# A third gate/up block multiplied plainly at the start of a float32 feed-forward layer

## The chip, the cores and the metric

The kernel runs on one core of a Trainium2 chip. A time is the device time of one execution in microseconds (us); of several runs the median is given. TensorE (PE in the profile) multiplies, PEld is its weight load, VectorE is DVE, ScalarE is ACT, GpSimd is POOL, and SyncE (SP) issues the loads of the weights.

## The reference, cut to what matters

One encoder layer on 512 tokens of width 2048 (forgetting attention, then a SwiGLU layer of inner width 5632), all in float32:

```
h = rmsnorm(x, norm_mix);  x = x + forgetting_attention(h)
h = rmsnorm(x, norm_ffn)
gu = h @ w_gate_up                    # 2048 x (2*5632)
x = x + (silu(gu[:, :5632]) * gu[:, 5632:]) @ w_down
out = rmsnorm(x, final_norm)
```

Only the line of `gu` is touched, and of it only the first 512 of the 5632 columns on each side.

## The kernel before, in words

Every float32 operand is held as a high and a low part in a rounded format. ScalarE copies the source into the high part, VectorE subtracts that from the source to get the low part, and TensorE adds three products: high by high, low by high, high by low. So each product of K-tiles is 3 matmuls, and each weight must pass through ScalarE and then VectorE before TensorE has the whole of it.

The feed-forward layer goes over 44 blocks of 128 inner columns, in 11 groups of 4. A group multiplies its four gate/up blocks and then adds the group's share of the down projection (16 output tiles, 192 matmuls of 512 columns). Groups 1 to 9 are a loop over `r`; group 0 is written out before it (`r is None`), the last behind it.

A block can be multiplied in three ways.
- `early` (L1604): block 0. Gate and up, each for one half of the tokens at a time, 48 matmuls of 256 columns. It needs nothing but the split weights in the two ring slabs of the phase before.
- `plain_part` (L1611): block 1. The block is cut into 4 parts (gate or up, first or second half of K); each part is 24 matmuls of 512 columns, 16 with the high weights and 8 with the low ones. 96 matmuls in all.
- `unit` with `half_product` (L1647, L1626): blocks 2 and 3, and every block of the later groups. The 2x2 form with seven products instead of eight. Weights B11, B12 (gate, up, first half of K) and B21, B22 (second half), tokens A11, A12, A21, A22 likewise. Each of the seven is 24 matmuls of 256 columns, so 168 in a unit. VectorE forms sums of weights in place in `raw` (`sum_of`), and the token sums S1 to S4 are formed once, before the first unit.

The token sums are made in pieces of 512 columns, four pieces for each: `sum_piece(i)` (VectorE from L1345, ScalarE from L944) makes piece i of S1, S2 and S3 and takes six additions or subtractions (L1338) and three low parts (L1343); ScalarE makes the high parts in between (L948, L950, L953). `fourth_piece(i)` makes piece i of S4 with 3 additions, a high part (L960) and a low part. All go through the same small tiles `sy`, `sz` and `qq`, so VectorE and ScalarE hand each piece back and forth.

The parts of the weights stand in a ring of two: part n may be written as a high part (ScalarE, L853, `part_hi`) once TensorE has read the highs of part n-2 (`highs_read`), as a low part (VectorE, L1217, `part_lo`) once part n-2 is done (`product`). The first two parts of the ring lie where block 0's gate slab was, and wait for `slab_used` of that slab. The raw weights come by loads of 512 KB into six slots of `raw` (`LOADS_0`, `load_units`).

Each engine executes its own list in the order it is written. What sets the order at the start of the layer are the lists of calls ahead of `group(None, 0)` on VectorE and ScalarE; TensorE goes block 0 (`early`), block 1 (4 plain parts), unit 2, unit 3, down. The first unit's product 1 needs all of S1, its product 2 all of S2, its product 3 all of S4.

Of the kernel before, what the change touches and what calls it, by code (L numbers as in the profile page):

```python
# [23 lines left out]
ALU = mybir.AluOpType  # L24
# [3 lines left out]
P = 128  # L28
# [34 lines left out]
G0_PARTS, G_PARTS = 26, 36  # L63
G0_PRODUCTS, G_PRODUCTS = 22, 32
G0_HIGHS, G_HIGHS = 18, 28
# [8 lines left out]
class Unit:  # L74
# [5 lines left out]
    def __init__(self, r, u):  # L80
        self.r, self.u = r, u
        self.nth = u - 2 if r is None else u
        self.first = 4 + 7 * self.nth if r is None else 7 * u
# [7 lines left out]
    def sums(self, j):  # L91
        return counted(8, 16, self.r, 4 * self.nth + j)

    def combined(self, j):
        return counted(8, 16, self.r, 4 * self.nth + j)

    def copied(self, j):
        return counted(4, 8, self.r, 2 * self.nth + j)

    def silu(self, j):  # L100
        return 2 + 2 * self.nth + j if self.r is None else 8 * self.r + (6 + 2 * self.nth + j)

    def act(self):
# [4 lines left out]
LOADS_0 = {("B11", 2): (0, 1), ("B12", 2): (1, 1), ("B22", 2): (4, 2), ("B21", 2): (5, 2),  # L108
           ("B11", 3): (2, 2), ("B12", 3): (3, 2), ("B22", 3): (4, 3), ("B21", 3): (5, 3),
           ("gate", 0): (2, 1), ("gate", 1): (3, 1), ("up", 0): (4, 1), ("up", 1): (5, 1),  # L110
# [12 lines left out]
def fox_layer(nc, x, norm_mix, w_in, b_f, w_out, norm_ffn, w_gu, w_down, norm_out, out):  # L123
# [34 lines left out]
    with ExitStack() as ctx:  # L158
# [97 lines left out]
        def bank_of(u, which):  # L256

            return (PROJ + PVB)[(u + which) % 4]
# [5 lines left out]
        def ring(part, n):  # L264

            return split[part][:, 0, (n % 2) * PART:(n % 2 + 1) * PART]
# [31 lines left out]
        def units(r):  # L298

            return [Unit(r, u) for u in range(2 if r is None else 0, G)]  # L300
# [171 lines left out]
        def _(sp):  # L472
# [35 lines left out]
            def load_part(r, name, i):  # L508

                n, _ = place(r, name, i)  # L510
                if name == "down":
                    cb, second = divmod(i, 2)
                    k = 2 * second if r is None else G * r + (G + 2 * second)
                    source = w_down_v[:, bass.ds(k, 2), cb * BANK:(cb + 1) * BANK]
                    view = slot(n).rearrange("p (k n) -> p k n", n=BANK)
                else:
                    if r is None and name in ("gate", "up"):
                        up, second, u = name == "up", i, 1
                    else:
                        up, second, u = name in ("B12", "B22"), name in ("B21", "B22"), i  # L520
                    col = u * P + up * F if r is None else (G * P) * r + (G * P + u * P + up * F)
                    source = w_gu_v[:, QK8 * second:QK8 * second + QK8, bass.ds(col, P)]
                    view = slot(n).rearrange("p (k n) -> p k n", n=P)
                sp.dma_start(view, source).then_inc(part_in[n], 16)

            def load_units(r):

                every = units(r)
                if r is None:
                    sp.wait_ge(lo_ready, FIRST_FFN)  # L530
                    load_part(r, "gate", 0)
                    load_part(r, "gate", 1)
                    sp.wait_ge(lo_ready, FIRST_FFN + 1)
                    load_part(r, "up", 0)
                    load_part(r, "up", 1)
                    sp.wait_ge(lo_ready, FIRST_FFN + 2)
                    load_part(r, "B11", 2)
                    load_part(r, "B12", 2)
                    for n, (name, u) in enumerate((("B11", 3), ("B12", 3), ("B22", 2), ("B21", 2))):
                        sp.wait_ge(t_lo, n + 1)  # L540
                        load_part(r, name, u)
# [129 lines left out]
        def _(act):  # L671
# [166 lines left out]
            def part_hi(r, n, source):  # L838

                if n >= 2:  # L840
                    if n - 2 < n_unit_parts(r):
                        act.wait_ge(highs_read, highs(r, n - 1))
                    elif n % 2 == 0:
                        act.wait_ge(product, products_done(r, n_unit_parts(r) + (n - n_unit_parts(r)) // 2))
                    else:
                        act.wait_ge(y_done, y_before(r) + NT * ((n - n_unit_parts(r)) // 2))
# [6 lines left out]
                nc.scalar.activation(ring(0, n), source, ACT.Copy).then_inc(t_hi, 1)  # L853
# [14 lines left out]
            def copy_q(at, j):  # L868
# [3 lines left out]
                nc.scalar.activation(qq[:, j * HALF:(j + 1) * HALF], ps[:, bank_of(at.u, j), 0:HALF],  # L872
# [7 lines left out]
            def gate_two(at):  # L880

                act.wait_ge(product, at.product(6))
                nc.scalar.activation(ga[:, HALF:S], ps[:, bank_of(at.u, 0), 0:HALF], ACT.Silu).then_inc(silu_done, 1)
# [6 lines left out]
            def unit(at, before, then):  # L890
# [5 lines left out]
                if before:  # L896
                    act_hi(at.r, before.u, ga[:, :])
# [64 lines left out]

            for i in range(3):
                sum_piece(i)
            plain_hi(None, 0, "gate", 0)
            plain_hi(None, 1, "gate", 1)
            sum_piece(3)
# [8 lines left out]
            plain_hi(None, 4, "B11", 2)  # L976
            fourth_piece(2)
            fourth_piece(3)
            sum_hi(Unit(None, 2), 1)

            act.wait_ge(product, 4)
            act.wait_ge(s_lo, 12)
# [22 lines left out]
        def _(dve):  # L1005
# [195 lines left out]
            def part_lo(r, n, source):  # L1201
# [15 lines left out]
                nc.vector.tensor_tensor(ring(1, n), source, f32(ring(0, n)), ALU.subtract).then_inc(t_lo, 1)  # L1217
# [30 lines left out]
            def bank(at, which):  # L1248
                return ps[:, bank_of(at.u, which), 0:HALF]

            def act_out(r, f, count):

                dve.wait_ge(silu_done, count)
                nc.vector.tensor_tensor(ga[:], ga[:], cc[:], ALU.mult).then_inc(a_done, 1)

# [6 lines left out]
            def unit(at, before, then):  # L1262
# [3 lines left out]
                if before:  # L1266
                    act_out(at.r, before.u, before.silu(2))
                unit_lo(at, 2)
                if before:
                    act_lo(at.r, before.u, ga[:])  # L1270
                elif at.r is None:
                    act_lo(None, 0, ga[:])
                    act_lo(None, 1, cc[:])
                    dve.wait_ge(a_ready, 2)
                unit_lo(at, 3)
                dve.wait_ge(t_sum, at.sums(2))
# [92 lines left out]
            def fourth_piece(i):  # L1369

                c = slice(i * S, (i + 1) * S)
                dve.wait_ge(s_lo, 12 + i)
                step(qq[:], f32(A12[0][:, c]), f32(A12[1][:, c]), ALU.add)
                dve.wait_ge(s_sum, 24 + 3 * i + 1)
                step(qq[:], qq[:], f32(S2[0][:, c]), ALU.add)
                dve.wait_ge(s_sum, 24 + 3 * i + 2)
                step(qq[:], qq[:], f32(S2[1][:, c]), ALU.add)
                low(S4[1][:, c], qq[:], f32(S4[0][:, c]), 12 + i + 1)


            dve.wait_ge(hT_done, 4 * NT * 2)
            for i in range(3):
                sum_piece(i)
            named_lo(None, 0, "gate", 0)
            named_lo(None, 1, "gate", 1)
            sum_piece(3)
            third_low(3)
            dve.wait_ge(silu_done, 1)
            wait_used(dve, At(FIRST_FFN + 1))
            nc.vector.tensor_tensor(ga[:], ps[:, GU[0][1], :], ga[:], ALU.mult).then_inc(a_done, 1)  # L1390
            named_lo(None, 2, "up", 0)
            fourth_piece(0)
            named_lo(None, 3, "up", 1)
            fourth_piece(1)
            unit_lo(Unit(None, 2), 0)
            first_sum(Unit(None, 2))
            fourth_piece(2)
            fourth_piece(3)
            dve.wait_ge(silu_done, 2)
            dve.wait_ge(product, 4)  # L1400
            nc.vector.tensor_tensor(cc[:], ps[:, GU[1][1], :], cc[:], ALU.mult).then_inc(a_done, 1)
# [16 lines left out]
        def _(pe):  # L1418
# [192 lines left out]
            def plain_part(n, bank, second):  # L1611

                pe.wait_ge(t_hi, n + 1)
                out = ps[:, bank, :].rearrange("p (h t) -> p h t", t=HALF)
                for k in range(QK8):
                    for part in range(2):
                        ins = nc.tensor.matmul(out, ring(0, n)[:, k * P:(k + 1) * P], h_ffn[part][:, :, QK8 * second + k, :],
# [3 lines left out]
                for k in range(QK8):  # L1621
                    ins = nc.tensor.matmul(out, ring(1, n)[:, k * P:(k + 1) * P], h_ffn[0][:, :, QK8 * second + k, :],
# [3 lines left out]
            def half_product(at, e):  # L1626
# [3 lines left out]
                out = ps[:, bank_of(at.u, which), 0:HALF]  # L1630
                fresh = which or e == 0
                pe.wait_ge(t_hi, at.part(e))
                for k in range(QK8):
                    for part in range(2):
                        ins = nc.tensor.matmul(out, ring(0, n)[:, k * P:(k + 1) * P],  # L1635
# [5 lines left out]
                for k in range(QK8):  # L1641
                    ins = nc.tensor.matmul(out, ring(1, n)[:, k * P:(k + 1) * P],  # L1642
# [4 lines left out]
            def unit(at):  # L1647

                first = at.r is None and at.nth == 0
                if first:  # L1650
                    pe.wait_ge(silu_done, 1)
# [3 lines left out]
                if first:  # L1655
                    pe.wait_ge(a_done, 1)
# [6 lines left out]
                if first:  # L1663
                    pe.wait_ge(silu_done, 2)
# [6 lines left out]
                if first:  # L1671
                    pe.wait_ge(a_done, 2)
# [11 lines left out]
            def down(r, cb, second, tb):  # L1684
# [3 lines left out]
                                lambda part, k: ring(part, n)[:, (k - 2 * second) * BANK:(k - 2 * second + 1) * BANK],  # L1688
# [29 lines left out]
            for n in range(4):  # L1718
                plain_part(n, GU[1][n // 2], n % 2)
# [50 lines left out]
```

## Time and profile before

| | us |
|---|---|
| median of 3 runs | 1839.42 (1839.38 to 1840.31) |
| the profiled execution | 1841.1 |
| its span in the trace | 1839.3 |
| TensorE busy | 1807.1 (98%) |
| VectorE busy | 1115.5 (61%) |
| ScalarE busy | 659.0 (36%) |

Busy time of TensorE counts overlapping, modelled ends of matmuls; how close it is to its rate is read from the distance of one matmul's start to the next one's. In a row of a timeline the first number is the start in us from the span's start, the second how long the merged instructions took, and brackets hold idle time before and what ended it. The granted clock (PEclk, 1.00 is 2.4 GHz, 0.50 is 1.2 GHz) is a mean over the stretch.

### The profile page before, as it was taken

To read this page: it belongs to the slowest core of one execution; us is meant where nothing else is said; L and a number is where in the kernel's file an instruction comes from. 1 tells how busy PE (TensorE), PEld (TensorE's weight loads), DVE (VectorE), ACT (ScalarE), POOL (GpSimd) and SP (SyncE) were. 2 spreads that over 40 slices of the span, in tenths; PEclk is the share of its full clock that TensorE was granted. 3 is DMA by queue.
4 is the path that set the end of the run, shared out by engine and by line. 5 is a ranking of instruction groups with operands and counts; after the bars stand their busy time and mean duration, and the time that the engine had idled before them with its cause. 6 is when DMAs were issued, how large, how long until landed. Compare 5 with 4: busy or idle time off the path is not lost.

```text
span 1839.3 us, 29804 instructions
## 1 busy us (share of the span) xinstructions
PE 1807.1 (98%) x11560; PEld 1647.4 (90%) x11560; DVE 1115.5 (61%) x1277; ACT 659.0 (36%) x867; POOL 58.5 (3%) x82
## 2 busy tenths in 40 slices
PE   8999999999799999999999999999999999999998
PEld 6888888888698999989989999899899899998996
DVE  5332432337875766757757667577477575674774
ACT  5232232334342433424424324234243243342444
POOL 3000000004000000000000000000000000000005
PEclk9999999999899999999999999999999999999999
DMA  7323322332133432343333333323333333234332
GB/s 229 87 75 92 91 68 91 143 132 69 46 93 100 115 118 82 93 127 94 102 93 101 112 109 93 117 81 120 98 92 104 104 115 108 77 110 119 92 138 92
DMA packets 268389, 189.55 MB, mean 103 GB/s; under 512 B 7280, under 2 KB 236656, under 8 KB 267376
## 3 DMA queue, kind: packets, MB, share of 16 engines
q1 hardware_dynamic: 265872, 181.46, 33.7%
q10 hardware_dynamic: 2400, 6.29, 0.9%
q8 instruction: 103, 1.69, 0.4%
q14 instruction: 14, 0.11, 0.0%
HBM read 183.54 MB, written 4.19 MB: 102 GB/s over the span
## 4 chain that ended last, share of the span: by engine, by line
PE 92%; DVE 4%; ACT 2%; issue 1%; POOL 1%; DMA 0%; ACTq 0%; POOLq 0%; DVEq 0%
PE ps L1423 45%; PE ps L1635 31%; PE ps L1642 15%; DVE tmp L1027 1%; DVE hT_lo L1015 1%; DVE qq L1338 1%; POOL xres L656 0%; DVE sy L1338 0%; PE ps L1436 0%; DVE oT_lo L1343 0%; ACT split_hi L853 0%; DMA xres<-in_x_dram 0%; DVE split_lo L1217 0%; DVE split_lo L1008 0%; PE ps L1478 0%
## 5 line engine op out<-in xcount | busy, mean ns | idle before, releaser
L853 ACT ACTIVATE split_hi<-raw 128x1024 fp32r<-128x1024 f32 x378 | 399.9, 1058 | 781.8 <-DVE raw L1231 387.7
L1217 DVE TENSOR_TENSOR split_lo<-raw,split_hi 128x1024 fp32r<-128x1024 f32 x378 | 462.0, 1223 | 331.5 <-ACT split_hi L853 331.5
L1423 PE MATMUL ps<-split_hi,hT_hi 128*128 128x512 f32 x704 | 274.2, 389 | 1.0 <-DVE hT_lo L1259 1.0
L1423 PE MATMUL ps<-split_lo,hT_hi 128*128 128x512 f32 x704 | 274.0, 389 | 0.0
L1423 PE MATMUL ps<-split_hi,hT_lo 128*128 128x512 f32 x704 | 273.9, 389 | 0.0
L1635 PE MATMUL ps<-hT_hi,split_hi 128*128 128x256 f32 x1008 | 247.8, 284 | 0.0
L1635 PE MATMUL ps<-hT_lo,split_hi 128*128 128x256 f32 x1008 | 247.3, 283 | 0.0
L1231 DVE TENSOR_TENSOR raw<-raw 128x1024 f32<-128x1024 f32 x168 | 205.2, 1221 | 9.6
L1635 PEld LDWEIGHTS ps<-hT_hi,split_hi 128*128 128x128 f32 x1008 | 193.4, 192 | 2.2 <-issue 2.0
L1635 PEld LDWEIGHTS ps<-hT_lo,split_hi 128*128 128x128 f32 x1008 | 193.4, 192 | 0.1
L1423 PE MATMUL ps<-hT_hi,split_hi 128*128 128x512 f32 (+1 forms) x464 | 171.2, 369 | 0.8 <-DVE split_lo L1008 0.8
L1635 PE MATMUL ps<-oT_hi,split_hi 128*128 128x256 f32 x672 | 166.4, 285 | 4.8 <-ACT split_hi L853 4.8
L1423 PE MATMUL ps<-hT_hi,split_lo 128*128 128x512 f32 (+1 forms) x464 | 170.4, 367 | 0.0
L1423 PE MATMUL ps<-hT_lo,split_hi 128*128 128x512 f32 (+1 forms) x464 | 170.4, 367 | 0.0
L1635 PE MATMUL ps<-oT_lo,split_hi 128*128 128x256 f32 x672 | 166.0, 284 | 0.0
L1163 DVE TENSOR_TENSOR xres<-ps,xres 128x512 f32<-128x512 f32 x192 | 126.5, 685 | 62.4 <-PE ps L1423 62.4
L1423 PEld LDWEIGHTS ps<-split_hi,hT_hi 128*128 128x128 f32 x704 | 132.2, 188 | 28.6 <-DVE hT_lo L1259 1.4
L1423 PEld LDWEIGHTS ps<-split_hi,hT_lo 128*128 128x128 f32 x704 | 132.2, 188 | 27.5
L1423 PEld LDWEIGHTS ps<-split_lo,hT_hi 128*128 128x128 f32 x704 | 132.2, 188 | 27.0
L1008 DVE TENSOR_TENSOR split_lo<-raw,split_hi 128x2048 fp32r<-128x2048 f32 x34 | 77.9, 2291 | 119.6 <-ACT split_hi L676 119.6
L1642 PE MATMUL ps<-hT_hi,split_lo 128*128 128x256 f32 x1008 | 141.5, 283 | 0.0
L1635 PEld LDWEIGHTS ps<-oT_hi,split_hi 128*128 128x128 f32 x672 | 129.6, 193 | 5.1 <-issue 5.0
(173 smaller groups left out, 2594.3 us busy)
## 6 DMA issues: line engine op xcount, KB each, us to landing
raw<-in_ffn_w_gate_up_dram SPq DMA_DIRECT2D x172, 512.0 KB, 4.2
raw<-in_ffn_w_down_dram SPq DMA_DIRECT2D x80, 512.0 KB, 4.1
raw<-in_fox_w_in_dram SPq DMA_DIRECT2D x24, 1024.0 KB, 5.7
raw<-in_fox_w_out_dram SPq DMA_DIRECT2D x8, 1024.0 KB, 5.1
xres<-in_x_dram SPq DMA_DIRECT2D x4, 1024.0 KB, 8.2
xres<-in_x_dram ACTq DMA_DIRECT2D x4, 1024.0 KB, 8.5
raw<-in_ffn_w_down_dram SPq DMA_DIRECT2D x4, 1024.0 KB, 5.6
out_dram<-xres SPq DMA_DIRECT2D x16, 256.0 KB, 3.1
```

The source lines that it names most:

```text
L853: nc.scalar.activation(ring(0, n), source, ACT.Copy).then_inc(t_hi, 1)
L1008: nc.vector.tensor_tensor(split[1][:, at.ring, :], raw[:, at.raw, :], f32(split[0][:, at.ring, :]), ALU.subtract).then_inc(lo_ready, 1)
L1015: nc.vector.tensor_tensor(turned_to(1, norm, tb, q), ps[:, turned(norm, tb, q)[0], :].rearrange("p (c t) -> p c t", t=P), f32(turned_to(0, ...
L1027: nc.vector.scalar_tensor_tensor(tmp[:, q, :], y(tb, q), rstd[:, tb:tb + 1], gain[:, q * BANK:(q + 1) * BANK], ALU.mult, ALU.mult).then_in ...
L1163: nc.vector.tensor_tensor(part, ps[:, bank, :], part, ALU.add).then_inc(added, 1)
L1217: nc.vector.tensor_tensor(ring(1, n), source, f32(ring(0, n)), ALU.subtract).then_inc(t_lo, 1)
L1231: nc.vector.tensor_tensor(x1, x1, x2, ALU.add).then_inc(t_sum, 1)
L1338: nc.vector.tensor_tensor(out, in0, in1, op).then_inc(s_sum, 1)
L1423: ins = nc.tensor.matmul(bank, stationary(sp, t), moving(mp, t), start=first and t == tiles[0] and (sp, mp) == PASSES[0], stop=last and t ...
L1635: ins = nc.tensor.matmul(out, ring(0, n)[:, k * P:(k + 1) * P], tokens[part][:, k * HALF:(k + 1) * HALF], start=bool(fresh) and k == 0 and ...
L1642: ins = nc.tensor.matmul(out, ring(1, n)[:, k * P:(k + 1) * P], tokens[0][:, k * HALF:(k + 1) * HALF], start=False, stop=k == QK8 - 1, ski ...
```

## The change

TensorE now multiplies blocks 1 and 2 plainly (8 plain parts, n = 0 to 7) and only block 3 of group 0 as a unit, so group 0 has 15 parts with products of gate and up instead of 18, and 23 parts in place of 26. Block 2's products go to the banks of block 0, so `plain_part` waits at n = 4 for block 0's gate to be read (`silu_done`) and at n = 6 for its up (`a_done`). Block 2's activation goes to a free half of raw slot 0 (`third`), and the load of the second down part into that slot waits until it has been split (`a_ready`). On VectorE and ScalarE the lists ahead of `group(None, 0)` are written anew: the parts of the plain blocks stand between the pieces of the token sums.

```diff
-G0_PARTS, G_PARTS = 26, 36
-G0_PRODUCTS, G_PRODUCTS = 22, 32
-G0_HIGHS, G_HIGHS = 18, 28
+PLAIN = 3
+G0_PARTS, G_PARTS = 23, 36
+G0_PRODUCTS, G_PRODUCTS = 19, 32
+G0_HIGHS, G_HIGHS = 15, 28
...
+                    for part in range(3):
+                        sp.wait_ge(lo_ready, FIRST_FFN + part)
+                        load_part(r, "plain", 2 * part)
+                        load_part(r, "plain", 2 * part + 1)
+                    for n, name, i in ((1, "B11", 3), (2, "B12", 3), (3, "plain", 6), (4, "plain", 7),
+                                       (6, "down", 0), (7, "B22", 3), (8, "B21", 3)):
+                        sp.wait_ge(t_lo, n)
+                        load_part(r, name, i)
+                    sp.wait_ge(a_ready, PLAIN)
+                    load_part(r, "down", 1)
...
             def part_hi(r, n, source):
                 if n >= 2:
+                    if r is None and n < 9:
+                        act.wait_ge(t_lo, n - 1)
...
+            sum_piece(0)
+            plain_hi(None, 0, "plain", 0)
+            plain_hi(None, 1, "plain", 1)
+            sum_piece(1)
+            plain_hi(None, 2, "plain", 2)
+            sum_piece(2)
             wait_used(act, At(FIRST_FFN))
             nc.scalar.activation(ga[:], ps[:, GU[0][0], :], ACT.Silu).then_inc(silu_done, 1)
-            plain_hi(None, 2, "up", 0)
+            sum_piece(3)
             fourth_piece(0)
-            plain_hi(None, 3, "up", 1)
+            plain_hi(None, 3, "plain", 3)
             act.wait_ge(product, 2)
             nc.scalar.activation(cc[:], ps[:, GU[1][0], :], ACT.Silu).then_inc(silu_done, 1)
             fourth_piece(1)
-            plain_hi(None, 4, "B11", 2)
+            plain_hi(None, 4, "plain", 4)
             fourth_piece(2)
+            plain_hi(None, 5, "plain", 5)
             fourth_piece(3)
...
+            sum_piece(0)
+            named_lo(None, 0, "plain", 0)
+            named_lo(None, 1, "plain", 1)
+            sum_piece(1)
+            sum_piece(2)
+            named_lo(None, 2, "plain", 2)
             sum_piece(3)
             third_low(3)
...
+            plain_out(0, ga[:])
+            for i in range(4):
+                fourth_piece(i)
+                named_lo(None, 3 + i, "plain", 3 + i)
+                fourth_low(i)
+            plain_out(1, cc[:])
+            named_lo(None, 7, "plain", 7)
+            unit_lo(Unit(None, 3), 0)
+            first_sum(Unit(None, 3))
...
             def plain_part(n, bank, second):
                 pe.wait_ge(t_hi, n + 1)
+                if n == 4:
+                    pe.wait_ge(silu_done, 1)
+                if n == 6:
+                    pe.wait_ge(a_done, 1)
...
-            for n in range(4):
-                plain_part(n, GU[1][n // 2], n % 2)
+            for n in range(8):
+                plain_part(n, GU[(n // 4 + 1) % 2][n // 2 % 2], n % 2)
```

In the unit of group 0, VectorE also gets the third block's product of gate and up (`plain_out(2, third)`) and its low part for the down projection, and ScalarE that one's high part; before, blocks 0 and 1 had these there, and block 2's were those of a unit.

ScalarE, from the end of the first token piece (`oT_hi` are the highs of S1 and S2, `s_hi` those of S3, `split_hi<-raw` a high part of weights, `split_hi<-qq` one of S4, `ga` the gate of block 0). Before:

```order
L953 ACTIVATE s_hi<-qq 128x512
L948 ACTIVATE oT_hi<-sy 128x512
L950 ACTIVATE oT_hi<-sy 128x512
L953 ACTIVATE s_hi<-qq 128x512
L853 ACTIVATE split_hi<-raw 128x1024 x2
L948 ACTIVATE oT_hi<-sy 128x512
L950 ACTIVATE oT_hi<-sy 128x512
L953 ACTIVATE s_hi<-qq 128x512
L969 ACT_TABLE_LOAD
L969 ACTIVATE ga<-ps 128x512
L853 ACTIVATE split_hi<-raw 128x1024
L960 ACTIVATE split_hi<-qq 128x512
```

The first pair of weight parts stood behind three pieces there, and part 2 directly behind the gate of block 0. Now, from the same place:

```order
L858 ACTIVATE split_hi<-raw 128x1024 x2
L955 ACTIVATE oT_hi<-sy 128x512
L957 ACTIVATE oT_hi<-sy 128x512
L960 ACTIVATE s_hi<-qq 128x512
L858 ACTIVATE split_hi<-raw 128x1024
```

The first pair has moved ahead of pieces 1 to 3, and part 2 stands behind piece 1. Behind piece 2, from the gate of block 0 on, ScalarE now has:

```order
L976 ACT_TABLE_LOAD
L976 ACTIVATE ga<-ps 128x512
L955 ACTIVATE oT_hi<-sy 128x512
L957 ACTIVATE oT_hi<-sy 128x512
L960 ACTIVATE s_hi<-qq 128x512
L967 ACTIVATE split_hi<-qq 128x512
L858 ACTIVATE split_hi<-raw 128x1024
```

The last row, part 3, stands behind all of piece 3 and the first piece of S4.

VectorE, from the last low part of S3 on (`split_lo<-raw` is a low part of weights, `split_lo<-qq` one of S4, `ga` and `cc` the activations of blocks 0 and 1). Before:

```order
L1343 TENSOR_TENSOR s_lo<-qq,s_hi 128x512
L1390 TENSOR_TENSOR ga<-ps,ga 128x512
L1217 TENSOR_TENSOR split_lo<-raw,split_hi 128x1024
L1338 TENSOR_TENSOR qq<-hT_hi,hT_lo 128x512
L1338 TENSOR_TENSOR qq<-qq,oT_hi 128x512
L1338 TENSOR_TENSOR qq<-qq,oT_lo 128x512
L1343 TENSOR_TENSOR split_lo<-qq,split_hi 128x512
L1217 TENSOR_TENSOR split_lo<-raw,split_hi 128x1024
```

Now:

```order
L1367 TENSOR_TENSOR s_lo<-qq,s_hi 128x512
L1274 TENSOR_TENSOR ga<-ps,ga 128x512
L1362 TENSOR_TENSOR qq<-hT_hi,hT_lo 128x512
L1362 TENSOR_TENSOR qq<-qq,oT_hi 128x512
L1362 TENSOR_TENSOR qq<-qq,oT_lo 128x512
L1228 TENSOR_TENSOR split_lo<-raw,split_hi 128x1024
L1367 TENSOR_TENSOR split_lo<-qq,split_hi 128x512
```

A low part of weights (parts 3 to 6 in turn) now stands inside each piece of S4, between its additions and its low part, and none between the last low part of S3 and the first piece of S4.

## Rows read from the trace of the kernel before

**Rows 1.** The page: span, busy share of TensorE, chain by engine.
```profile
span 1839.3 us, 29804 instructions
PE 1807.1 (98%) x11560; PEld 1647.4 (90%) x11560; DVE 1115.5 (61%) x1277; ACT 659.0 (36%) x867; POOL 58.5 (3%) x82
PE 92%; DVE 4%; ACT 2%; issue 1%; POOL 1%; DMA 0%; ACTq 0%; POOLq 0%; DVEq 0%
```

**Rows 2.** Waits of TensorE: line, waited for, us in total, times, longest.
```profile
PE ps L1617 <- ACT split_hi L853: 7.5, 1, 7.5
PE ps L1635 <- ACT split_hi L853: 4.8, 1, 4.8
```

**Rows 3.** Chain that ended last, in time: start, us, instructions; second unit and first down.
```profile
519.56 1.92 PE ps L1635 x16
522.44 1.92 PE ps L1635 x16
...
542.60 43.55 PE ps L1423 x192
```

**Rows 4.** Timeline of TensorE from the end of block 0 on.
```profile
463.71 0.28 PE L1423 MATMUL ps<-hT_hi,split_lo 128*128 128x256 f32 x1
471.53 0.79 PE L1617 MATMUL ps<-hT_hi,split_hi 128*128 128x512 f32 x1 [7.54 <-ACT split_hi L853]
...
477.44 1.98 PE L1622 MATMUL ps<-hT_hi,split_lo 128*128 128x512 f32 x8
...
503.43 0.53 PE L1635 MATMUL ps<-oT_hi,split_hi 128*128 128x256 f32 x1 [4.83 <-ACT split_hi L853]
...
506.93 1.11 PE L1642 MATMUL ps<-oT_hi,split_lo 128*128 128x256 f32 x8
```

**Rows 5.** Timeline of VectorE: pieces of token sums and low parts.
```profile
456.88 0.69 DVE L1338 TENSOR_TENSOR sy<-hT_hi,hT_lo 128x512 f32<-128x512 f32 x1
...
462.64 0.69 DVE L1343 TENSOR_TENSOR oT_lo<-sy,oT_hi 128x512 fp32r<-128x512 f32 x1
463.37 0.69 DVE L1338 TENSOR_TENSOR sy<-hT_hi,hT_lo 128x512 f32<-128x512 f32 x1
...
471.51 2.36 DVE L1217 TENSOR_TENSOR split_lo<-raw,split_hi 128x1024 fp32r<-128x1024 f32 x2 [1.70 <-ACT split_hi L853]
473.79 0.69 DVE L1338 TENSOR_TENSOR sy<-hT_hi,hT_lo 128x512 f32<-128x512 f32 x1
...
479.41 0.69 DVE L1343 TENSOR_TENSOR oT_lo<-sy,oT_hi 128x512 fp32r<-128x512 f32 x1
480.86 0.69 DVE L1343 TENSOR_TENSOR s_lo<-qq,s_hi 128x512 fp32r<-128x512 f32 x1 [0.76 <-ACT s_hi L953]
...
484.86 0.68 DVE L1338 TENSOR_TENSOR qq<-hT_hi,hT_lo 128x512 f32<-128x512 f32 x1
```

**Rows 6.** Timeline of ScalarE: highs of weights and of S4, the gate.
```profile
470.44 1.99 ACT L853 ACTIVATE split_hi<-raw 128x1024 fp32r<-128x1024 f32 x2
...
480.85 1.28 ACT L969 ACT_TABLE_LOAD   x1
...
487.03 0.63 ACT L960 ACTIVATE split_hi<-qq 128x512 fp32r<-128x512 f32 x1 [3.34 <-DVE qq L1338]
487.57 1.04 ACT L853 ACTIVATE split_hi<-raw 128x1024 fp32r<-128x1024 f32 x1
```

**Rows 7.** Windows: stretch, length, busy us per engine, granted clock, DMA share, GB/s.
```profile
440.00:450.00 10.00, 9.37 (x76) 8.66 (x75) 9.27 (x10) 6.02 (x11) 4.85 (x3) 1.00 0.67 181
450.00:460.00 10.00, 10.00 (x86) 10.00 (x85) 9.49 (x16) 2.34 (x5) 0.00 (x0) 1.00 0.01 2
...
464.00:471.50 7.50, 0.00 (x0) 0.00 (x0) 5.41 (x9) 2.92 (x6) 0.00 (x0) 0.63 0.00 0
471.50:477.00 5.50, 5.47 (x15) 4.33 (x16) 5.42 (x7) 1.37 (x2) 0.00 (x0) 0.58 0.54 149
477.00:484.00 7.00, 7.00 (x32) 5.80 (x31) 4.46 (x8) 4.28 (x6) 0.00 (x0) 1.00 0.12 35
```

More of the change, by code:

```diff
@@ L298, in units @@
         def units(r):
-            return [Unit(r, u) for u in range(2 if r is None else 0, G)]
+            return [Unit(r, u) for u in range(PLAIN if r is None else 0, G)]
         x_in = [sem(f"x_in{i}") for i in range(NT)]
@@ L516, in load_part @@
                 else:
-                    if r is None and name in ("gate", "up"):
-                        up, second, u = name == "up", i, 1
+                    if name == "plain":
+                        up, second, u = i % 4 >= 2, i % 2, 1 + i // 4
                     else:
@@ L896, in unit @@
                 if before:
-                    act_hi(at.r, before.u, ga[:, :])
+                    act_hi(at.r, at.u - 1, ga[:, :])
+                elif at.r is None:
+                    act_hi(None, 2, third)
                 plain_hi(at.r, at.first + 3, "B22", at.u)
@@ L975, in _ @@
             fourth_piece(1)
-            plain_hi(None, 4, "B11", 2)
+            plain_hi(None, 4, "plain", 4)
             fourth_piece(2)
+            plain_hi(None, 5, "plain", 5)
             fourth_piece(3)
-            sum_hi(Unit(None, 2), 1)
-            act.wait_ge(product, 4)
-            act.wait_ge(s_lo, 12)
+            plain_hi(None, 6, "plain", 6)
+            plain_hi(None, 7, "plain", 7)
+            act.wait_ge(product, 6)
+            nc.scalar.activation(third, ps[:, GU[0][0], :], ACT.Silu).then_inc(silu_done, 1)
+            plain_hi(None, 8, "B11", 3)
+            sum_hi(Unit(None, 3), 1)
+            act.wait_ge(product, 8)
             act_hi(None, 0, ga[:])
@@ L1254, in act_out, with plain_out @@
                 nc.vector.tensor_tensor(ga[:], ga[:], cc[:], ALU.mult).then_inc(a_done, 1)
+            def plain_out(f, into):
+                dve.wait_ge(silu_done, f + 1)
+                if f:
+                    dve.wait_ge(product, 4 * f)
+                else:
+                    wait_used(dve, At(FIRST_FFN + 1))
+                nc.vector.tensor_tensor(into, ps[:, GU[f % 2][1], :], into, ALU.mult).then_inc(a_done, 1)
             def act_lo(r, f, source):
@@ L1275, in unit @@
                 unit_lo(at, 3)
+                if at.r is None:
+                    act_lo(None, 2, third)
                 dve.wait_ge(t_sum, at.sums(2))
@@ L1616, in plain_part @@
                     for part in range(2):
-                        ins = nc.tensor.matmul(out, ring(0, n)[:, k * P:(k + 1) * P], h_ffn[part][:, :, QK8 * second + k, :],
+                        ins = nc.tensor.matmul(out, ring(None, 0, n)[:, k * P:(k + 1) * P], h_ffn[part][:, :, QK8 * second + k, :],
                                                start=second == 0 and k == 0 and part == 0, stop=False)
@@ L1629, in half_product @@
                 n = at.first + e
-                out = ps[:, bank_of(at.u, which), 0:HALF]
+                out = ps[:, bank_of(at, which), 0:HALF]
                 fresh = which or e == 0
@@ L1647, in unit @@
             def unit(at):
-                first = at.r is None and at.nth == 0
+                first = at.r is None
                 if first:
-                    pe.wait_ge(silu_done, 1)
+                    pe.wait_ge(silu_done, 2)
                 else:
```

100 lines of the change are left out of this document (36 added, 64 removed).

## The prediction

> **What bounds the kernel now.** I read the page first: TensorE is busy 98% of the span and holds 92% of the chain that ended last [rows 1]. So time comes off only where TensorE idles, runs at the lower clock, or has fewer matmuls. Then the waits of TensorE alone: two stand out, both for a high part of weights from ScalarE, 7.5 and 4.8 us [rows 2]. The timeline puts them at the start of the feed-forward layer: after block 0 until 471.53, and between products 0 and 1 of the first unit until 503.43 [rows 4]. The windows show what follows: the granted clock is 0.63 in the idle stretch and 0.58 in the 5.5 us behind it, then 1.00 again [rows 7]. A full-rate matmul of 512 columns takes 43.55 / 192 = 0.2268 us, a product of 24 matmuls of 256 columns 522.44 - 519.56 = 2.88 us [rows 3]; behind the first wait the 16 high matmuls took 477.44 - 471.53 = 5.91 us instead of 3.63, 2.28 lost; behind the second, 506.93 - 503.43 = 3.50 instead of 1.92, 1.58 lost [rows 4].
>
> The stretch in figures. Block 0's last matmul starts at 463.71, so the next could at 463.83; the first down of group 0 starts at 542.60 [rows 3, 4], 78.77 us later. The work in it is 4 x 5.44 (a plain part is 24 x 0.2268) + 14 x 2.88 = 62.1. The rest, 16.7, is 7.70 + 2.28 for the first wait, and about 5.0 + 1.58 for the second (product 0 ends at 477.44 + 8 x 0.2268 + 3 x 5.44 + 2.88 = 498.45); some 0.15 is left over.
>
> **What the change does to the work.** A unit of 7 x 2.88 = 20.16 us is replaced by 4 x 5.44 = 21.77: 1.6 us more for TensorE, on the path, so 63.7 us in the stretch. The most that the change can bring is thus 16.7 - 1.6 = 15.1 us, with no idle and no low clock left.
>
> Here a rule of the Trainium skill speaks against the change: "TensorE: Matmul & The Clock Gate", section Back-to-back issue gap, gives N / 2.4 + 2.5 ns for one matmul to the next. By it a plain block would be 96 x 215.8 ns = 20.7 us and a unit 168 x 109.2 ns = 18.3 us, an added 2.4 us instead of 1.6, and the forecast 0.8 us later. The rows, 0.2268 and 0.120 us [rows 3], disagree with it here, and the sum goes by them.
>
> **The first wait.** The high parts 0 and 1 stood behind three token pieces. Now they stand behind one, and wait for block 0's gate slab, released when its second 48 matmuls end: 463.83 - 48 x 0.12 = 458.07, some 458.3 with the way to ScalarE. One high part later TensorE could start; it is busy with block 0's up until 463.83. The loads are the same six of 512 KB in the same slots under the same conditions; the DMA share falls from 0.67 to 0.01 at 450 [rows 7], so data is there. The first wait goes, with its low clock. What is late next?
>
> **Laying VectorE's and ScalarE's lists end to end.** From the rows of like instructions:
> - High part to low part: 471.51 - 470.44 = 1.07, so the first low part starts at 459.4. Two low parts: 473.79 - 471.51 = 2.28, so piece 1 starts at 461.65 [rows 5, 6].
> - A piece that follows a low part has its last low of S2 5.62 after its start (479.41 - 473.79), 5.76 without one ahead (462.64 - 456.88) [rows 5]. The next piece starts 0.73 later: piece 2 at 468.0. Its last low at 473.75, low part 2 at 474.4, piece 3 at 474.4 + 1.14 = 475.5.
> - Piece 3 ends with S3's last low, 480.86 - 473.79 = 7.07 after its start [rows 5]: at 482.6. Block 0's activation 483.25, first addition of S4 483.95 (0.69 each).
> - From that addition to S4's high part 487.03 - 484.86 = 2.17, and 0.54 more to the high part of weights behind it [rows 5, 6]: high part 3 starts at 486.6, and TensorE 1.09 later (471.53 - 470.44, rows 4 and 6), at 487.7.
>
> ScalarE's table load (1.28 [rows 6]) now falls between pieces 2 and 3, about 475 to 477; ScalarE has nothing from VectorE until 475.5 + 2.9, so it costs nothing. High part 2 follows piece 1 at about 468.9, long before its use at 474.7. TensorE, starting at 463.83, has done parts 0, 1 and 2 at 463.83 + 3 x 5.44 = 480.16. It then waits for high part 3 until 487.7: **a new wait of 7.5 us**, because one whole piece of S1 to S3 and one of S4 stand ahead of that part on both engines. The added `t_lo` wait of ScalarE is for low part 1 or 2, done before: nothing.
>
> **Low clock.** The new wait is as long as the first one was (7.54 [rows 4]), behind which 2.28 us were lost, and shorter ones lost 1.58. I take 2.28; the ends are 0 (rival B) and staying low (rival E). The same page of the Trainium skill, section What's actually happening, says that the number of slow matmuls behind an idle stretch varies from run to run; by it this term could differ between executions, which one profiled execution can't show.
>
> **Parts 4 to 7.** Each turn of the loop on VectorE and ScalarE is 2.17 + 0.54 + 1.07 for S4's additions and highs, 1.14 for the low part and 0.73 for S4's low: 5.65 us against 5.44 for a part. Part 3 ends at 487.7 + 5.44 + 2.28 = 495.4; high part 4 can be used at 486.6 + 5.65 + 1.09 = 493.3. The margin is 2.1 us and shrinks by 0.2 a turn, so parts 4, 5 and 6 don't wait. Without the 2.28 of low clock they would, by some 0.6 in all: the low clock costs 1.7 net. Part 7's highs follow directly. The waits for `silu_done` and `a_done` at parts 4 and 6 are for work of 477 and 484, long done. S4 is complete at about 507, its use starts at about 526.
>
> **Unit 3.** The high of its product 1 needs the highs of part 7 read, about 3 us before its use; as with every unit. S1 to S4 are all there, so the second wait (5.0 + 1.58) goes wholly. VectorE has three low parts of activations and one multiplication more than a unit before (4 x 0.69), and has finished its sums before the unit starts, so these lie beside TensorE's 20.16 us. SP now waits for the third activation before it loads the second down part; behind that wait stand the other down loads, none of which could start earlier than the sum that follows it on VectorE, and TensorE needs the part some 15 us later against 4 to 5 for a load. From the first down on everything is as before, and TensorE is the chain, so the whole shift reaches the end.
>
> **Sum.** 463.83 + 63.7 + 7.54 + 2.28 + 0.1 = 537.4 against 542.6: 5.2 us less. The profiled execution of 1841.1 becomes 1835.9; it lies 1.7 above the median 1839.42, so the forecast is 1834.2.
>
> **Rivals.**
> - A, the forecast: wait of about 7.5 at part 3 with low clock behind it; 1833.4 to 1835.0. Chance 0.73.
> - B, no low clock behind the wait, or a short one: 1.7 less, 1832.5. Against it: both waits of the kernel before had it. 0.09.
> - C, the parts between the sums keep TensorE fed, as the words of the change have it: 15.1 less, 1824.3. It would need high part 3 by 479, when ScalarE is still in piece 3. 0.05.
> - D, the turns of parts 4 to 6 take longer than laid out, since low parts and additions mix there as nowhere in the rows: each us more a turn costs up to 1 per part beyond the margin of 2. At 7 us a turn the three turns come to 3 x 1.56 less 2.1, 2.6 more: 1836.8, no measurable change. 0.10.
> - E, slower: the clock doesn't come back behind the new wait but stays at the lower level. There 24 matmuls of 512 columns take 24 x 0.427 = 10.2 us (0.427 = twice 0.2133, the 512 columns at 1.2 GHz; the clock of 0.58 over 471.5 to 477 [rows 7] is near this level), 4.8 more a part. It outweighs the 5.2 after about one more slow part and is slower by over 0.2% after two; with three, 1848.6. Against it: the clock was 1.00 from 477 on [rows 7]. 0.03.
>
> **How the numbers follow.** The likeliest is A, 1834.2. The range takes in A and B and half of D, 1832.0 to 1836.5; C and E and the far end of D are left out. A measurement of this kernel can tell 0.2%, 3.7 us, from no change, so faster means below 1835.7: A, B, C and a small part of D, 0.88. Same: most of D, 0.09. Slower: E, 0.03.
>
> **What would show it.** Right: one wait of TensorE for a high part, 7 to 8 us long, ended near 487.7, in the plain parts (between the 72nd and 73rd of their matmuls); a granted clock near 0.6 in the 5 us behind it; no wait at 464 and none between products 0 and 1 of the unit; first down of group 0 near 537.4, and all behind it shifted by the same 5.2. Wrong: waits at parts 4 to 6 too (D), high part 3 at 479 (C), or a clock below 1.00 after 493 (E).

## The result and the profile after

The changed kernel takes 1851.55 us (median of 6 runs, 1847.92 to 1854.93), the kernel before 1840.43 beside it: a ratio of 1.0059, interval 1.0046 to 1.0072. It is 11.1 us slower where 5.2 us less was forecast. The interval lies wholly above 1. The profiled execution took 1852.24 us, its span in the trace is 1850.4; what is said below of single stretches is of that one execution unless another is named.

First the page of the changed kernel: the span, the engines, and the granted clock in tenths of full speed over 40 slices of the span.

```profile
span 1850.4 us, 29653 instructions
...
PE 1814.4 (98%) x11488; PEld 1648.5 (89%) x11488; DVE 1105.0 (60%) x1266; ACT 655.4 (35%) x861; POOL 58.7 (3%) x82
...
PEclk9999999999998999999999999999999999999999
```

TensorE has 72 matmuls fewer and 7.3 us more of busy time than in [rows 1]. The one slice below 9 is the 13th, 555 to 601 us; in the kernel before it was the 11th, 460 to 506. Its waits (line, waited for, us in total, times, longest) answer to [rows 2]:

```profile
PE ps L1448 <- DVE xres L1174: 9.5, 3, 3.2
PE ps L1646 <- ACT split_hi L858: 7.3, 1, 7.3
```

The second of these is the new wait at plain part 3, as forecast. The first is new and not in the prediction: three waits of 3.2 us each, in the down projection. The chain of waits (start, us, what) shows where, as against one row of 43.55 us in [rows 3]:

```profile
536.79 10.92 PE ps L1448 x48
550.85 12.77 PE ps L1448 x48
566.76 14.02 PE ps L1448 x48
583.93 13.94 PE ps L1448 x48
```

These are the four column blocks of group 0's down projection. The first starts at 536.79, 5.8 us earlier than before. The next group's first matmul follows at 597.87 instead of 586.15 (542.60 + 43.55), 11.7 us later. So the down projection took 61.1 us instead of 43.55, **17.5 us more**. A group later the shift is still 11.75 (678.51 against 666.76) and at the end of the span 11.1; the last 0.6 is left open.

What ScalarE does in that stretch says why. Its timeline (start, us, instruction, idle before and what ended it):

```profile
547.79 2.00 ACT L858 ACTIVATE split_hi<-raw 128x1024 fp32r<-128x1024 f32 x2 [8.04 <-PE ps L1448]
563.70 2.00 ACT L858 ACTIVATE split_hi<-raw 128x1024 fp32r<-128x1024 f32 x2 [13.91 <-PE ps L1448]
580.87 2.00 ACT L858 ACTIVATE split_hi<-raw 128x1024 fp32r<-128x1024 f32 x2 [15.16 <-PE ps L1448]
```

It writes the highs of a column block in pairs, each time only after TensorE's last matmul of the block before. In the kernel before they went one at a time, each 5.44 us, half a column block, behind the one before:

```profile
553.60 1.06 ACT L853 ACTIVATE split_hi<-raw 128x1024 fp32r<-128x1024 f32 x1 [4.38 <-PE ps L1423]
559.04 1.06 ACT L853 ACTIVATE split_hi<-raw 128x1024 fp32r<-128x1024 f32 x1 [4.38 <-PE ps L1423]
```

The ring holds two parts, and a slot is free as soon as the half block that used it is done. Here the first of a pair waits for the whole block, although its slot has been free for half of it. VectorE's order comes on top: it writes the low part first and then adds four output tiles, and TensorE needs the first of those tiles' banks. So a wait is 1.07 for the high part, 1.14 for the low part, one addition of 0.69, and the ways between, 3.14 in all. The list of waits names only the one that ended last, the addition on VectorE.

The line that decides it is in `part_hi` (from L841 in the changed kernel, L838 before) and, with `dve` in place of `act`, in `part_lo` (from L1212, L1201 before):

```
if n - 2 < n_unit_parts(r):
    act.wait_ge(highs_read, highs(r, n - 1))
elif n % 2 == 0:
    act.wait_ge(product, products_done(r, n_unit_parts(r) + (n - n_unit_parts(r)) // 2))
else:
    act.wait_ge(y_done, y_before(r) + NT * ((n - n_unit_parts(r)) // 2))
```

In the down projection `product` counts the first halves of the column blocks, `y_done` the tiles of whole blocks. Which of them frees a slot goes by whether the part is a first or a second half, that is by `n - n_unit_parts(r)`; the code asks for `n` itself. With 18 or 28 unit parts that is the same. The change makes it 15 in group 0, and the two releases swap: each first half waits for `y_done`, the whole block before. Each second half waits for too little, only the first half of the block before. That does no harm here, since on each engine it stands behind the first half, which has waited for the whole block. The change did adapt the ring's addresses to the odd count (`ring`), but not this.

### The profile page after: what moved, and what is told of

Same layout as the page of the kernel before. It is cut to its first block, busy times and chain, and to the rows that moved or that the text cites. A ratio compares the mean times of both kernels' runs of the same rounds, so it can differ in the third digit from the quotient of the medians.

```text
span 1850.4 us, 29653 instructions
## 1 busy us (share of the span) xinstructions
PE 1814.4 (98%) x11488; PEld 1648.5 (89%) x11488; DVE 1105.0 (60%) x1266; ACT 655.4 (35%) x861; POOL 58.7 (3%) x82
## 4 chain that ended last, share of the span: by engine, by line
PE 93%; DVE 3%; ACT 1%; issue 1%; POOL 1%; DMA 0%; ACTq 0%; POOLq 0%; DVEq 0%
PE ps L1448 46%; PE ps L1664 30%; PE ps L1671 15%; PE ps L1646 1%; DVE tmp L1038 1%; POOL xres L659 0%; PE ps L1651 0%; DVE hT_lo L1026 0%; PE ps L1461 0%; DVE xres L1174 0%; DVE sy L1362 0%; ACT split_hi L858 0%; DMA xres<-in_x_dram 0%; DVE split_lo L1019 0%; PE ps L1503 0%
## 5 line engine op out<-in xcount | busy, mean ns | idle before, releaser
L1664 PE MATMUL ps<-hT_hi,split_hi 128*128 128x256 f32 x984 | 241.5, 283 | 0.0
L1664 PE MATMUL ps<-hT_lo,split_hi 128*128 128x256 f32 x984 | 241.4, 283 | 0.0
L1242 DVE TENSOR_TENSOR raw<-raw 128x1024 f32<-128x1024 f32 x164 | 200.5, 1222 | 9.5
L1664 PEld LDWEIGHTS ps<-hT_hi,split_hi 128*128 128x128 f32 x984 | 188.8, 192 | 1.3 <-issue 0.9
L1664 PEld LDWEIGHTS ps<-hT_lo,split_hi 128*128 128x128 f32 x984 | 188.8, 192 | 0.3
L1664 PE MATMUL ps<-oT_hi,split_hi 128*128 128x256 f32 x656 | 160.9, 283 | 0.0
L1664 PE MATMUL ps<-oT_lo,split_hi 128*128 128x256 f32 x656 | 160.7, 283 | 0.0
L1671 PEld LDWEIGHTS ps<-hT_hi,split_lo 128*128 128x128 f32 x984 | 126.9, 192 | 0.0
```

Source lines behind the costliest of these rows:

```text
L1242: nc.vector.tensor_tensor(x1, x1, x2, ALU.add).then_inc(t_sum, 1)
L1664: ins = nc.tensor.matmul(out, ring(at.r, 0, n)[:, k * P:(k + 1) * P], tokens[part][:, k * HALF:(k + 1) * HALF], start=bool(fresh) and k == ...
L1671: ins = nc.tensor.matmul(out, ring(at.r, 1, n)[:, k * P:(k + 1) * P], tokens[0][:, k * HALF:(k + 1) * HALF], start=False, stop=k == QK8 - ...
```

## Experiments

All ratios are to the kernel before, run beside them on the same chip: median 1840.57 for e1 to e4, 1840.62 for e5 to e8.

### The releases, mended in the changed kernel

```diff
-                    elif n % 2 == 0:
+                    elif (n - n_unit_parts(r)) % 2 == 0:
```

(in `part_hi` and in `part_lo`)

> The changed kernel, with one edit: in the down projection the condition that picks a ring slot's release goes by the part's number within the down projection, (n - n_unit_parts(r)) % 2, and no longer by n % 2. Theory P (the odd count of 15 unit parts in group 0 swaps the two releases, so that high part 2 of each pair waits for a whole column block): the down projection of group 0 takes 43.6 us instead of 60.9 in the trace, no wait of TensorE is left in it, and the time is 5.2 us under the kernel before (0.9972), 17 under the changed kernel. Theory L (the weights of the down projection land late, since SP now waits for the third activation ahead of them): the edit changes nothing, the time stays some 11 us above the kernel before (1.006).

Measured: 1835.22 us (1833.29 to 1836.38, 5 runs), ratio 0.9966, interval 0.9952 to 0.9979. The chain of waits has the down projection whole again:

```profile
537.89 43.55 PE ps L1448 x192
```

Theory P holds, theory L (late loads) falls: the loads are issued under the same conditions as in the changed kernel. What is left is 5.35 us under the kernel before, where the forecast had 5.2. So the stretch that the prediction laid out came out in sum as forecast; its single terms are compared further down.

### The releases, swapped in the kernel before

```diff
-                    elif n % 2 == 0:
+                    elif (n % 2 == 0) != (r is None):
```

(in both; the down projection of group 0 only)

> The kernel before, with only the two releases swapped in the down projection of group 0, and all loads, blocks and lists as they were. Theory P: three waits of TensorE of 3.2 us each and the low clock behind them, as in the changed kernel, and the time is 15 to 18 us above the kernel before (1.008 to 1.010). Theory L: no more than 1 us, since the loads and their waits are those of the kernel before.

Measured: 1855.07 us (1853.78 to 1858.27, 4 runs), ratio 1.0075, interval 1.006 to 1.0091, which is 14.5 us more, just under the 15 to 18 expected; its profiled run, the longest, is 17.2 over that of before. Waits of TensorE:

```profile
PE ps L1423 <- DVE xres L1163: 9.5, 3, 3.2
PE ps L1617 <- ACT split_hi L853: 7.5, 1, 7.5
PE ps L1635 <- ACT split_hi L853: 4.8, 1, 4.8
```

The same three waits of 3.2 us appear beside the two of [rows 2], and the column blocks behind them take 12.77, 13.92 and 13.91 us, within 0.1 of those of the changed kernel. Nothing else of the change is needed for the loss.

### What part of the loss is the clock

A column block without a disturbance is 43.55 / 4 = 10.89 us. Between the blocks of the chain above are 3.14, 3.14 and 3.15 us, 9.4 in all. The other 8.1 are in the blocks themselves: 12.77, 14.02 and 13.94 are 1.9, 3.1 and 3.1 more than 10.89. Not all of that need be the clock. Windows of the changed kernel (stretch, length, busy us per engine, granted clock, DMA share, GB/s):

```profile
547.70:550.90 3.20, 0.05 (x1) 0.08 (x1) 2.02 (x3) 2.00 (x2) 0.00 (x0) 1.00 0.00 0
550.90:563.70 12.80, 12.71 (x48) 10.02 (x48) 2.73 (x4) 0.00 (x0) 0.00 (x0) 0.87 0.59 164
...
566.80:580.90 14.10, 13.97 (x48) 10.92 (x48) 2.74 (x4) 0.03 (x1) 0.00 (x0) 0.79 0.26 74
...
584.00:597.90 13.90, 13.90 (x50) 11.25 (x51) 6.95 (x9) 1.06 (x1) 0.00 (x0) 0.79 0.27 77
```

To test it, TensorE got work to do in the waits:

```diff
+                    if r is None and cb < NC - 1:
+                        keep_busy(14, PVB[1])
```

(`keep_busy` issues matmuls of A11 by itself, 512 columns each, whose result is used by nothing)

> The changed kernel with the swapped releases left in, and 14 matmuls of 512 columns more on TensorE behind each of the first three column blocks of group 0's down projection (14 x 0.2268 = 3.2 us, as long as each of the three waits; their result is used by nothing). The 17.5 us that the down projection took more are 3 x 3.4 us of waiting and 1.9 + 3.1 + 3.1 us of low clock by the trace. If the low clock comes from the idle stretches, it goes: the time is 7 to 8 us under e8 (the changed kernel beside it), and a column block takes 10.9 us again. Rival: TensorE's clock falls there for another reason, and the time is within 2 us of e8's or up to 1 us over.

Measured: 1845.04 us (1844.05 to 1845.39, 7 runs), ratio 1.0027, interval 1.0016 to 1.0037, 6.5 under the changed kernel beside it (1851.54, run e8 below), against 7 to 8 expected. The granted clock is 1.00 through the whole stretch. The blocks behind the added matmuls take 11.13 to 11.15 us, not the 10.9 expected:

```profile
536.92 10.91 PE ps L1448 x48
547.83 3.17 PE ps L1640 x14
551.00 11.13 PE ps L1448 x48
562.13 3.17 PE ps L1640 x14
565.30 11.15 PE ps L1448 x48
```

So 0.25 us in each block is not low clock: it is there at a clock of 1.00. In this trace 0.08 of it is the longer way from the first matmul to the second, and some 0.16 is how the chain counts the end of the last matmul. With 11.13 to 11.15 as the measure, the low clock cost 1.6, 2.9 and 2.8 us in the changed kernel. The whole down projection says the same: 53.85 us here (536.92 to 590.77) against 61.1 there. The 17.5 us of that execution are thus 9.4 us of waiting, 0.8 at the edges of the blocks, and 7.3 of low clock that the idle stretches bring. The expectation's 3 x 3.4 + 1.9 + 3.1 + 3.1 is 18.3 and counts the edges twice. Added matmuls that compute nothing make the changed kernel faster, though it stays 4.4 us over the kernel before.

> The changed kernel again, beside the others on the same chip: 1848 to 1855 us, 8 to 15 over the kernel before. Its runs lay 7 us apart; if that spread comes from where the clock is low, e5 and e1, with no low clock in the down projection, spread less.

Measured: 1851.54 us (1845.97 to 1854.38, 6 runs), ratio 1.0054, interval 1.004 to 1.0069. The second guess held too: the changed kernel's runs lie 7.0 and 8.4 us apart, those of e5 1.3 and those of e1 3.1. The two traces of the changed kernel show one place where the spread comes from. In both, the three waits are of the same length. The block behind the first of them took 12.77 us in one (granted clock 0.87) and 14.08 in the other (0.78); the two later blocks agree within 0.02. So the waits of TensorE are the same in both, and what the clock takes behind them isn't: 7.3 us in one execution, 8.6 in the other.

### The release mended on one engine only

The same edit as in e1, in `part_hi` (ScalarE) alone.

> The changed kernel with the release in the down projection mended on ScalarE alone; VectorE's low parts keep the swapped one. The high part is then written early, but TensorE waits for the low part too, which still waits for the whole column block: each of the three waits is shorter by one high part, about 1.1 us, so 3 to 4 us under e8, and the low clock behind them may be the same or partly gone. If ScalarE's release were the whole cause, it would be 17 us under e8.

Measured: 1843.34 us (1842.47 to 1845.33, 10 runs), 8.2 under e8 where 3 to 4 were expected. The waits are shorter by what was expected:

```profile
PE ps L1448 <- DVE xres L1174: 6.2, 3, 2.1
```

That is 3.3 us less in all, and VectorE's release indeed still holds the low part back. The rest is the clock: the blocks behind the waits took 11.17, 11.18 and 12.76 us here, against 12.77, 14.02 and 13.94. The first two are e5's blocks at full clock, and the granted clock is 1.00 in both:

```profile
549.20 11.17 PE ps L1448 x48
...
562.44 11.18 PE ps L1448 x48
...
575.68 12.76 PE ps L1448 x48
```

```profile
549.20:560.40 11.20, 11.16 (x48) 8.90 (x48) 2.77 (x4) 1.06 (x1) 0.00 (x0) 1.00 0.66 188
...
562.40:573.60 11.20, 11.16 (x48) 8.93 (x48) 2.82 (x4) 1.06 (x1) 0.00 (x0) 1.00 0.32 94
...
575.70:588.40 12.70, 12.70 (x50) 10.32 (x50) 6.93 (x9) 1.06 (x1) 0.00 (x0) 0.87 0.29 84
```

So the waits of 2.1 us cost nothing, nothing and 1.6 us of low clock, where those of 3.2 us cost 1.6, 2.9 and 2.8. My expectation left this open ("may be the same or partly gone") and gave no number for it.

### The new wait at part 3

```diff
             def plain_part(n, bank, second):
+                if n == 3:
+                    keep_busy(31, SC[1])
```

(on top of e1)

> e1_parity with 31 matmuls of 512 columns more on TensorE ahead of plain part 3, into a bank that is free then (31 x 0.2268 = 7.0 us); their result is used by nothing. The wait for high part 3 stays as long as it is, but TensorE has work in it. If the low clock behind the wait costs what the prediction says (2.28 us, of which 0.6 comes back as waits at parts 4 to 6), this is 1.7 us under e1_parity. If the low clock costs nothing on the path, it is the same as e1_parity or up to 0.5 us slower.

Measured: 1832.83 us (1832.35 to 1835.18, 5 runs), ratio 0.9963 (0.995 to 0.9976), 2.4 under e1 where 1.7 was expected. The two ranges of runs overlap, and with 5 runs each the difference isn't clear of the noise; the traces are the better witness. Within them, from the first plain part to the first down, it is 72.1 us (462.50 to 534.62) against 74.1 in e1 (463.80 to 537.89), 2.0 less. TensorE's wait at part 3 is down to 0.3. The windows of e1 show what was filled:

```profile
480.00:488.00 8.00, 0.71 (x3) 0.40 (x2) 5.44 (x9) 3.28 (x5) 0.00 (x0) 0.68 0.00 0
488.00:493.00 5.00, 5.00 (x13) 3.83 (x13) 3.49 (x5) 1.41 (x3) 0.00 (x0) 0.50 0.38 105
```

### The parts put in another order

On top of e1, the same calls in both lists in another order. ScalarE's, abbreviated to its calls (`h` high part of weights, `s` piece of S1 to S3, `q` piece of S4, `si` a gate's silu, `sh1` the first sum's high part):

```diff
-s0 h0 h1 s1 h2 s2 si0 s3 q0 h3 si1 q1 h4 q2 h5 q3 h6 h7 si2 h8 sh1
+s0 h0 s1 h1 s2 h2 h3 si0 s3 h4 q0 si1 h5 q1 q2 h6 h7 q3 h8 si2 sh1
```

and VectorE's (`l` low part of weights, `t3` last low of S3, `ql` low of S4, `po` a product of gate and up, `sum1` the first weight sum):

```diff
-s0 l0 l1 s1 s2 l2 s3 t3 po0 q0 l3 ql0 q1 l4 ql1 q2 l5 ql2 q3 l6 ql3 po1 l7 l8 sum1
+s0 s1 l0 s2 l1 l2 s3 l3 t3 q0 l4 ql0 q1 ql1 q2 po0 l5 ql2 q3 l6 l7 l8 po1 sum1 ql3
```

> e1_parity with the calls of both lists in another order, so that no plain part stands behind a whole piece of S3 and S4: ScalarE writes high part 3 right behind high part 2, ahead of piece 3, and high part 4 ahead of the first piece of S4; on VectorE likewise, with one low part of weights for each piece. If the wait at part 3 is only a matter of order, as the prediction's laying-out has it, TensorE has no wait over 1 us between block 0 and the first down, which starts at 527.6 instead of 536.8, and the time is 14 to 15 us under the kernel before (0.992). Rival: VectorE has too much to do in the stretch whatever the order, and the wait turns up at a later part or in front of the unit; then it is less than 8 us under.

Measured: **1825.24 us** (1824.43 to 1826.42, 5 runs), ratio 0.9916, interval 0.9902 to 0.9929, 15.3 us under the kernel before and some 26 under the changed one. TensorE has no wait between block 0 and the first down; the granted clock is 1.00 throughout:

```profile
464.00:500.00 36.00, 36.00 (x160) 29.83 (x159) 31.57 (x43) 15.44 (x20) 0.00 (x0) 1.00 0.30 88
500.00:527.50 27.50, 27.50 (x202) 26.22 (x202) 19.38 (x22) 12.35 (x16) 0.00 (x0) 1.00 0.37 115
```

The first down starts at 527.62, 63.9 us behind the first plain part, which is the 63.7 of the work itself. This is the 15.1 us that the prediction named as the most that the change can bring.

### Is the third block needed, or is it the order?

The kernel before with its two blocks, and only the order of the lists changed in the same way (ScalarE `s0 h0 s1 h1 s2 h2 s3 h3 si0 q0 si1 q1 h4 q2 sh1 q3`, VectorE `s0 s1 s2 l0 s3 l1 t3 q0 l2 ql0 po0 q1 l3 ql1 q2 l4 ql2 sum1 q3 po1 ql3`; high parts 2 to 4 wait for the low part two before them, as in the change).

> The kernel before, with its two blocks outside the units (0 and 1) and only the lists of VectorE and ScalarE in another order: the plain parts stand between the pieces of the token sums (ScalarE: piece 0, high 0, piece 1, high 1, piece 2, high 2, piece 3, high 3 and so on), as in e4 but without a third block multiplied plainly. If the gain of e4 is order alone, this is 15 to 17 us under the kernel before, since it has 1.6 us less of matmuls. If the third block is needed as work for TensorE while VectorE forms the sums, VectorE's own work (20 us of it before product 1 of the first unit) still leaves waits of 8 to 9 us in all, spread over parts 0 to 3 and the unit's first products: first down near 534.5, 8 us under the kernel before (0.9956), and 7 over e4.

Measured: 1833.77 us (1831.28 to 1834.91, 5 runs), ratio 0.9965, interval 0.9952 to 0.9978, 6.9 under the kernel before and 8.5 over e4. Its waits between block 0 and the first down:

```profile
PE ps L1634 <- DVE split_lo L1220: 3.4, 1, 3.4
PE ps L1647 <- ACT qq L874: 1.4, 1, 1.4
PE ps L1654 <- DVE split_lo L1220: 0.9, 1, 0.9
```

The waits are 5.7 us instead of the 8 to 9 expected, but low clock stands behind the first (0.50 in the window 469 to 474) and again near the end of them (0.86 from 495 to 500). The first down starts at 534.81, 72.9 us behind the first plain part, where the work is 62.1. So this order alone brings under half of e4's gain, and the third block serves as work for TensorE while VectorE forms the sums, though it makes TensorE's own work 1.6 us longer. Only this one order of the two-block kernel was run; that no other would do better is not shown.

## Why the prediction was wrong

**What bounds the kernel, and the ceiling:** right. 15.1 us at most; e4 took 15.3.

**Work added:** right by the rows. In e4 the stretch took 63.9 us against 63.7 worked out from 0.2268 and 2.88 us. By the formula of the Trainium skill that the prediction weighed ("TensorE: Matmul & The Clock Gate", section Back-to-back issue gap), which is given there for the gap of an isolated matmul, it would have been 8 x 24 x 0.2158 + 168 x 0.1092 = 59.8 us: too fast for both kinds of matmul, and 4 us off here.

**The first wait, and the laying-out of the lists:** right. The first wait went, and the new one at part 3 ended at 487.54 (forecast 487.7) and was 7.3 us long (7.5):

```profile
487.54 0.80 PE L1646 MATMUL ps<-hT_hi,split_hi 128*128 128x512 f32 x1 [7.30 <-ACT split_hi L858]
...
492.89 1.99 PE L1651 MATMUL ps<-hT_hi,split_lo 128*128 128x512 f32 x8
```

Behind it, the 16 high matmuls took 492.89 - 487.54 = 5.35 us instead of 3.63: 1.7 lost, 2.28 forecast. In e1 it was 2.7 (487.60 to 493.97), and in e8, the same kernel again, 2.8 (487.56 to 493.95). So this term varies from one execution to the next, and that 2.28 lies in the middle is in part luck. The Trainium skill says that the number of slow matmuls varies between runs of one kernel ("TensorE: Matmul & The Clock Gate", section What's actually happening). It says so of a kernel's start; the prediction carried it over to a wait, and the traces bear that out.

**Parts 4 to 7 and unit 3:** right. No wait there, no wait between products 0 and 1; the first down at 536.79, forecast 537.4 (537.89 in e1, 537.84 in e8). That parts 4 to 6 would run a little late without the low clock, by 0.6 in all, is near what e3 shows: their 16 high matmuls took 3.81, 3.87 and 3.81 us instead of 3.63.

**"From the first down on everything is as before, and TensorE is the chain, so the whole shift reaches the end":** this step failed. It was not worked out at all. The change replaces three counts (26, 22, 18 by 23, 19, 15), and I carried the counts along as bookkeeping, without asking what is computed from them. One of them decides by its parity which release a slot of the ring waits for. The sum for the stretch behind the edit should have had a term: first half waits for the whole block before, 3 times (1.07 + 1.14 + 0.69 and the ways between, 3.2), and then low clock behind each, 1.58 to 2.28 by [rows 4]. That gives 3 x 3.2 + 3 x 1.58 = 14.3 to 3 x 3.2 + 3 x 2.28 = 16.4 us, and with the 5.2 gained, 1848.6 to 1850.7. What the runs showed in place of "as before" is 17.5 us more in group 0's down projection, 9.4 of it waiting and 7.3 low clock (18.8 in e8's trace).

**Rivals:** none had this mechanism. The slower one (E, the clock stays low behind the wait at part 3) didn't happen: the clock was 1.00 from 496 to the first down. That its 1848.6 lies near the measured time is chance. C, in which the parts keep TensorE fed, describes what the change could have been; e4 shows it, at 1825.2 against 1824.3 worked out. B, a small cost of low clock behind the wait at part 3, fits none of the traces: it was 1.7 to 2.9. D (longer turns) didn't happen. The range (1832.0 to 1836.5) missed the time by 15 us and held that of e1.

**The last of the signs of being right, "all behind it shifted by the same 5.2",** was the one that told: shift at the first down -5.8, at the next group +11.7.

## What to carry to other kernels

When a change alters how many items pass through a ring, look up every place where such a count or an absolute number is tested by its remainder, on each engine; a condition that waits too long gives no wrong result and no hang, only time, and may stand in a stretch that the change doesn't touch. The other half of the swap waits for too little, and was harmless here only by the order on its engine. After the change compare the start of each later stage in both traces: where the shift changes sign or size is the place, and a wait named for VectorE's addition there was in truth a high part two steps back. Where TensorE must wait for lists of two other engines, lay the lists out end to end from like rows, and move calls until nothing that it needs stands behind a whole unit of what it doesn't.

## What was not expected of the hardware

The clock needn't fall during the wait. In the changed kernel the window 547.7 to 550.9, the first of the three waits, has the clock at 1.00, and so has the first us behind it; it falls only after that, while TensorE is at work:

```profile
551.00:552.00 1.00, 1.00 (x5) 0.82 (x6) 1.00 (x3) 0.00 (x0) 0.00 (x0) 1.00 0.62 168
552.00:553.00 1.00, 1.00 (x5) 0.83 (x4) 1.00 (x2) 0.00 (x0) 0.00 (x0) 0.68 0.86 266
553.00:554.00 1.00, 1.00 (x4) 0.72 (x4) 0.63 (x1) 0.00 (x0) 0.00 (x0) 0.50 0.24 90
```

In the two later waits it fell before TensorE went on (0.87 in the window 563.7 to 566.8, 0.85 from 580.9 to 584), and in e8 in all three (0.90, 0.87 and 0.87). So the granted clock of an idle window doesn't tell whether there is a price.

The price of a wait is also out of proportion to its length. The wait at part 3 (7.3 us) cost 1.7 (the changed kernel) to 2.9 us (e5) of low clock, two of the three waits of 3.2 us in the down projection some 2.9 each, and two of the three waits of 2.1 us in e7 nothing. Taking 1 us off each of the three waits (e7) brought 8.2 us. Finer windows of the changed kernel show how a short wait can cost more than a long one:

```profile
484.00:487.50 3.50, 0.00 (x0) 0.00 (x0) 1.81 (x3) 1.59 (x3) 0.00 (x0) 0.51 0.00 0
487.50:491.00 3.50, 3.46 (x8) 2.81 (x9) 3.38 (x5) 0.47 (x1) 0.00 (x0) 0.51 0.27 70
...
566.00:566.75 0.75, 0.00 (x0) 0.02 (x1) 0.75 (x3) 0.00 (x0) 0.00 (x0) 0.51 0.00 0
566.75:573.00 6.25, 6.24 (x15) 4.91 (x16) 2.79 (x4) 0.00 (x0) 0.00 (x0) 0.51 0.58 164
```

Both times the clock is low for some 7 us. Around part 3 half of that lies in the wait, where a low clock costs nothing, and half on matmuls. Around the second wait of the down projection nearly all of it lies on matmuls. Why the clock falls where it does, and why the low stretch behind the first wait was shorter in this execution than in e8's, is left open.
